# A delta-rule layer whose instructions are written in another order: the chain of the recurrence first, one shared PSUM bank in one fixed sequence

## The reference

```python
a = lmat + eye                       # per chunk, unit lower triangular; lmat from k k^T, decay, beta
sol = solve_triangular(a, rhs)       # rhs: beta v and beta k exp(g)
intra = where(tril, (q @ k.T) * decay, 0)
def step(state, inp):                # one chunk after the other
    v_new = uc - wc @ state
    out = (qc * exp(gc)) @ state + ac @ v_new
    state = state * exp(g_last) + (kc * exp(g_last - gc)).T @ v_new
    return state, out
o = o_fwd + o_bwd
o = o * rsqrt(mean(o * o) + EPS) * out_norm * silu(z)
```

## Time and profile before

| | us |
|---|---|
| three runs: lowest, median, highest | 2757.07, 2758.05, 2759.13 |
| the profiled execution | 2765.49 |
| its span, first to last instruction | 2763.5 |
| mean granted TensorE clock in it | 0.968 of full speed |
| the seven rounds of the delta layer, 2138.25 to 2338.00 | 199.8 |

### The profile page before, as it was taken

How to read it: one execution, slowest core, us unless ns; L and a number is a source line. 1 busy time by engine, 2 the same in 40 slices (tenths; PEclk the granted TensorE clock), 3 DMA queues, 4 the chain that set the end, 5 groups by cost and what they waited for, 6 DMA issues and landing times.

```text
span 2763.5 us, 32840 instructions
## 1 busy us (share of the span) xinstructions
PE 2574.3 (93%) x12894; PEld 2107.8 (76%) x12894; DVE 1379.9 (50%) x2344; ACT 1097.8 (40%) x1898; POOL 342.5 (12%) x535
## 2 busy tenths in 40 slices
PE   5979999999999989889999999999998888999998
PEld 3767777778766767778967888888776887888887
DVE  5667567466464655653234533325776434443322
ACT  4355342353353545444363422215544443422222
POOL 2233011001200013110000000001023520000000
PEclk9989999999999999999999999999998889999999
DMA  5522265246410421143201333334323000333332
GB/s 220 183 76 70 92 220 173 84 139 190 134 35 29 133 73 47 45 126 92 69 1 37 109 97 94 99 96 150 92 61 67 25 26 5 92 100 97 93 99 76
DMA packets 155521, 258.83 MB, mean 94 GB/s; under 512 B 20367, under 2 KB 73642, under 8 KB 154345
## 3 DMA queue, kind: packets, MB, share of 16 engines
q1 hardware_dynamic: 134992, 201.62, 23.2%
q0 software_dynamic: 18128, 53.46, 6.0%
q10 hardware_dynamic: 2249, 1.65, 0.2%
HBM read 249.78 MB, written 10.02 MB: 94 GB/s over the span
## 4 chain that ended last, share of the span: by engine, by line
PE 75%; DVE 10%; ACT 8%; DMA 3%; POOL 2%; issue 2%; SPq 0%; ACTq 0%; DVEq 0%; POOLq 0%
PE PS L219 19%; PE PS L220 19%; PE PS L221 19%; PE PS L979 2%; PE PS L1807 2%; ACT tmp L746 2%; PE PS L1584 1%; PE PS L1603 1%; PE PS L1823 1%; DVE dn_qkvT L2873 1%; DVE x L802 1%; DVE w_lo L211 1%; DVE macc L490 1%; DVE hT_lo L814 1%; PE PS L1593 1%
## 5 line engine op out<-in xcount | busy, mean ns | idle before, releaser
L204 ACT ACTIVATE w_hi<-w_raw 128x1024 fp32r<-128x1024 f32 (+1 forms) x348 | 357.8, 1035 | 1062.1 <-DMA w_raw<-in_ffn_w_gate_up 308.1
L211 DVE TENSOR_TENSOR w_lo<-w_raw,w_hi 128x1024 fp32r<-128x1024 f32 (+1 forms) x348 | 412.3, 1194 | 723.0 <-ACT w_hi L204 721.6
L219 PE MATMUL PS<-hT_hi,w_hi 128*128 128x512 f32 (+1 forms) x1600 | 611.4, 382 | 27.0 <-DVE hT_lo L814 18.9
L221 PE MATMUL PS<-hT_hi,w_lo 128*128 128x512 f32 (+1 forms) x1600 | 603.2, 377 | 0.0
L220 PE MATMUL PS<-hT_lo,w_hi 128*128 128x512 f32 (+1 forms) x1600 | 603.0, 377 | 0.0
L219 PE MATMUL PS<-w_hi,hT_hi 128*128 128x512 f32 (+1 forms) x864 | 349.7, 405 | 30.9 <-ACT gla_szT L1048 8.3
L219 PEld LDWEIGHTS PS<-hT_hi,w_hi 128*128 128x128 f32 x1600 | 307.7, 192 | 86.0 <-issue 25.2
L221 PEld LDWEIGHTS PS<-hT_hi,w_lo 128*128 128x128 f32 x1600 | 307.0, 192 | 54.3
L220 PEld LDWEIGHTS PS<-hT_lo,w_hi 128*128 128x128 f32 x1600 | 307.6, 192 | 51.9 <-issue 0.2
L220 PE MATMUL PS<-w_lo,hT_hi 128*128 128x512 f32 (+1 forms) x864 | 340.0, 394 | 0.0
L221 PE MATMUL PS<-w_hi,hT_lo 128*128 128x512 f32 (+1 forms) x864 | 339.5, 393 | 0.0
(11 more groups left out here) (610 smaller groups left out, 3459.5 us busy)
## 6 DMA issues: line engine op xcount, KB each, us to landing
w_raw<-in_ffn_w_gate_up SPq DMA_DIRECT2D x176, 256.0 KB, 3.1
mraw<-in_w_mod POOLq DMA_DIRECT2D x160, 256.0 KB, 3.9
w_raw<-in_gla_w_in SPq DMA_DIRECT2D x48, 512.0 KB, 4.6
w_raw<-in_ffn_w_down SPq DMA_DIRECT2D x44, 512.0 KB, 3.7
w_raw<-in_fox_w_in SPq DMA_DIRECT2D x32, 512.0 KB, 3.8
w_raw<-in_sgu_w_in SPq DMA_DIRECT2D x24, 512.0 KB, 4.9
w_raw<-in_dn_w_in SPq DMA_DIRECT2D x24, 512.0 KB, 3.8
w_raw<-in_gla_w_out SPq DMA_DIRECT2D x16, 512.0 KB, 4.5
```

The source lines that it names most:

```text
L204: nc.scalar.activation(w_hi[:, n % NS, :, 0:m], w_raw[:, n % NS, :, 0:m], ACT.Copy).then_inc(w_hidone, 1)
L211: nc.vector.tensor_tensor(w_lo[:, n % NS, :, 0:m], w_raw[:, n % NS, :, 0:m], w_hi[:, n % NS, :, 0:m].bitcast(F32), ALU.subtract).then_inc( ...
L219: nc.tensor.matmul(o, l_hi, r_hi, start=start, stop=False)
L221: return nc.tensor.matmul(o, l_lo, r_hi, start=False, stop=stop)
```

## The change

The arithmetic is the same. The loop bodies of PE, ACT and DVE are written in another order, the waits are fitted to it, and a few buffers move:

- The scores go to bank 7 instead of bank 1, which gives bank 7 one fixed sequence in a round: lengths and length rows of head h - 2, v turned, k turned, scores.
- In a round PE starts with hop 1 of chunk 0 and `right(h, 0)`; `decay_rows` moves from the first place to the middle, `scores` from third to near the end, behind `turn(h, 1)`. `right` no longer waits for `dn_AT`.
- The first `turn` takes banks 2 and 3 before `decay_rows` does; the second `turn` therefore waits for the two exponentials that read the decay rows there (`eg`).
- Lengths, square root and output of a head come one round later than before (head h - 2 in round h), the last head's behind the loop.
- The keys of the second direction are decayed on DVE (`decayed_key`, 4 instructions), no longer on ACT.
- The second inverse of heads 3 to 5 has a place of its own, so SP's load of it waits for the recurrence only at h = 2.
- POOL's order is unchanged; in `decayed_query` the count of `prep` becomes 3 h + 3, since the scores are now third to count there.

```diff
@@ positions and waits on PE
                 def decay_rows(h):
                     for d in range(2):
-                        if h:
-                            t_.wait_ge(q.te, B.te + 5 * h)
+                        t_.wait_ge(q.te, B.te + 5 * h + d + 1)
...
                 def scores(h):
-                    if h:
-                        t_.wait_ge(q.pc, B.pc + 4 * h)
+                    t_.wait_ge(q.kte, h + 1)
+                    t_.wait_ge(q.D, 3 * h + 3)
                     for c in range(TT):
-                        mm = t_.matmul(PS[:, 1, cs(c)], r.qkvT[:, HP + HO[h], cs(c)], ...
+                        mm = t_.matmul(PS[:, 7, cs(c)], r.qkvT[:, HP + HO[h], cs(c)], ...
...
-                            t_.wait_ge(q.at, 2 * h + 2)
+                            if h:
+                                t_.wait_ge(q.pc, B.pc + 4 * h)
...
+                            if n == 1:
+                                t_.wait_ge(q.eg, 2 * h + d + 1)
...
@@ PE, the loop
                 for h in range(NH + 1):
...
-                    if inv:
-                        decay_rows(h)
                     if rec:
-                        recur(h - 1, 0, 0)
                         recur(h - 1, 0, 1)
                     if inv:
-                        scores(h)
...
                         right(h, 0)
...
+                    if h >= 2:
+                        lengths(h - 2)
...
+                    if inv:
+                        decay_rows(h)
+                        turn_k(h)
+                    if rec:
+                        recur(h - 1, 2, 0)
+                    if inv:
+                        right(h, 1)
+                    if h == 0:
+                        chunk_matrix(5, (4, 5, 6))
...
+                    if inv:
+                        turn(h, 1)
+                    if rec:
                         recur(h - 1, 2, 2)
                     if inv:
-                        right(h, 1)
+                        scores(h)
...
@@ ACT, the loop
+                        a.wait_ge(q.prep, 3 * h + 2)
+                        for c in range(TT):
+                            ins = a.activation(r.qkvT[:, 2 * HP + HO[h], cs(c)], PS[:, 7, cs(c)], ...
+                        ins.then_inc(q.kte, 1)
+                        rows_exp(0)
                     if rec:
                         value_new(h - 1, 2)
                     if inv:
                         right_out(h, 1)
-                        turned_out(h, 1)
+                        rows_exp(1)
...
@@ POOL
                 def decayed_query(h):
...
-                    p.wait_ge(q.prep, 3 * h + 1)
+                    p.wait_ge(q.prep, 3 * h + 3)
...
@@ DVE, the loop
                     if rec:
                         state(h - 1, 0)
...
+                    if h >= 2:
+                        output(h - 2)
+                    if inv:
+                        decay(0)
+                    if rec:
+                        residual(h - 1, 2)
+                    if inv:
+                        decay(1)
+                        decayed_key()
...
+                    if inv:
+                        weights(1)
                         merge(h, 1)
                     if rec:
-                        output_lengths(h - 1)
+                        gated(h - 1)
+                length_recip(NH - 1)
+                normed(NH - 1)
                 output(NH - 1)
```

More of the change, by code:

```diff
@@ L2501, in recur @@
                         if hop == 0:
[L2502 to L2508, removed]
                             if c == 1 and d == 0:
@@ L2524, in recur @@
                         else:
+                            if c == 0 and d == 0:
+                                if h:
+                                    t_.wait_ge(q.oy, B.oy + 3 * h - 2)
+                                t_.matmul(PS[:, 6, :], r.zr[0:1, :], r.zr[0:1, 0:1].to_broadcast([1, S]), start=True, stop=False)
+                                t_.wait_ge(q.at, 2 * h + 2)
                             t_.wait_ge(q.ve, i + 1)
@@ L2636, in pe @@
                     if inv:
-                        turn(h, 1)
-                    if h == 0:
-                        chunk_matrix(5, (4, 5, 6))
+                        left(h, 1)
                     if rec:
@@ L2642, in pe @@
                     if inv:
-                        left(h, 1)
+                        turn(h, 2)
                     if rec:
                         recur(h - 1, 3, 2)
-                        lengths(h - 1)
-                    if inv:
-                        turn(h, 2)
-                    if rec:
-                        length_rows(h - 1)
+                lengths(NH - 1)
+                length_rows(NH - 1)
                 t_.wait_ge(q.os, B.os + KT)
@@ L2752, in act, with rows_exp, root @@
                     p = h % 2
-                    if inv:
-                        for d in range(2):
-                            a.wait_ge(q.D, 2 * h + d + 1)
-                            if d == 0 and h:
-                                a.wait_ge(q.qg, 2 * h)
-                            a.activation(ajunk[:] if d == 0 else qg_at(h), PS[:, 2 + d, :], ACT.Exp).then_inc(q.eg, 1)
+                    def rows_exp(d):
+                        a.wait_ge(q.D, 3 * h + d + 1)
+                        if d == 0 and h:
+                            a.wait_ge(q.qg, 2 * h)
+                        a.activation(ajunk[:] if d == 0 else qg_at(h), PS[:, 2 + d, :], ACT.Exp).then_inc(q.eg, 1)
+                    def root(n):
+                        a.wait_ge(q.head, 3 * n + 2)
+                        a.activation(stat[:, 40:44], PS[:, 7, 0:TT], ACT.Sqrt, scale=1.0 / P, bias=eps[:]).then_inc(q.root, 1)
                     if rec:
@@ L3012, in dve, with decay @@
                     p = h % 2
-                    if h >= 2:
-                        output(h - 2)
-                    if inv:
-                        for d in range(2):
-                            v.wait_ge(q.gr, 2 * h + d + 1)
-                            for c in range(TT):
-                                ins = v.scalar_tensor_tensor(out=d_.AT[:, p, d, cs(c)], in0=PS[:, 2 + d, cs(c)],
-                                                             scalar=r.G[:, d, c, HO[h]:HO[h] + 1], in1=r.cm[:, d, :],
-                                                             op0=ALU.subtract, op1=ALU.add)
-                            ins.then_inc(q.D, 1)
+                    def decay(d):
+                        v.wait_ge(q.gr, 2 * h + d + 1)
+                        for c in range(TT):
+                            ins = v.scalar_tensor_tensor(out=d_.AT[:, p, d, cs(c)], in0=PS[:, 2 + d, cs(c)],
+                                                         scalar=r.G[:, d, c, HO[h]:HO[h] + 1], in1=r.cm[:, d, :],
+                                                         op0=ALU.subtract, op1=ALU.add)
+                        ins.then_inc(q.D, 1)
@@ L3023, in dve @@
                     if rec:
                         state(h - 1, 0)
-                    if inv:
-                        v.wait_ge(q.prep, 3 * h + 1)
-                        for d in range(2):
-                            v.wait_ge(q.Dx, 2 * h + d + 1)
-                            v.tensor_tensor(d_.AT[:, p, d, :], d_.AT[:, p, d, :], PS[:, 1, :], ALU.mult).then_inc(q.at, 1)
+                    if h >= 2:
+                        length_recip(h - 2)
                     if rec:
                         residual(h - 1, 1)
-                        state(h - 1, 1)
-                        residual(h - 1, 2)
+                    if h >= 2:
+                        normed(h - 2)
```

122 lines of the change are left out of this document (70 added, 52 removed).

## The result

The changed kernel takes 2772.8 us (median of 5, 2767.1 to 2773.1); timed beside it, the one before takes 2758.05. The ratio is **1.0043, 95% interval [1.0025, 1.0061]**: 11.9 us slower, between 6.9 and 16.8. A second timing gave 1.0037 [1.0023, 1.0050]. Forecast: 2766.0 us, +8.0, slower.

A forecast was written before the change was run, and what follows sets the result against it. The chain runs through round 0 to POOL's transfers, POOL's solve, then PE's rounds 3 to 6 and tail. 9.6 - 4.8 + 3.3 = 8.1 us later; 2758.05 + 8.0 = 2766.0 us, range 2757.5 to 2773.5.

The forecast's parts named there:

- Part 1: Round 0, POOL's start: 24 block transfers wait behind decayed_query(0) for the scores, ending 9.6 us later.
- The bounds: Round 0's lateness: 9.1 us with PE at full clock from the start, 11.6 with underrated waits on ACT.
- Part 2: POOL's chain from last issue to toe keeps its 58.3 us; decayed_query(1) has 5 us of cover; right(3, 0) at 2248.6.
- Part 3: Rounds 3 to 5: 24.7 us each at full clock, plus slow-clock time; 4.8 of the 9.6 us won back.
- the wait that I had named: Mid-round on PE: turn(h, 1) waits for ACT's second decay exponential, costing 0.25 + 1.55 us.
- the 1.5 us for rounds 4 and 5: Slow-clock allowance on PE for rounds 4 and 5 together, 1.5 us.
- Part 4: Round 6 and tail: head 4's work now stands between the hops, +3.3 us, bounds 1.5 and 4.5; tail unchanged.
- its items: Round 6: square and product +1.0, lengths and length rows +0.9 and +0.8, output's cast and subtraction +0.6 us.
- rival 1: Rounds 3 to 5 have no slow stretches, round 6 costs half: +2.0 us, or 2760; chance 0.22.
- rival 2: Rounds don't get shorter, 27.8 us each, through ACT's middle wait or a hop: +12.9 us, 2771; chance 0.14.
- rival 3: POOL's solve is interrupted, waiting for round 1's scores, for instance 4 us: +12, 2770; chance 0.06.
- rival 4: The 24 issues don't hold the solve, issue and making overlap as before: -6.0 us, 2752; chance 0.04.

The follow-up runs named there:

- e1a: Changed kernel with POOL's 24 block transfers and load back ahead of decayed_query(0): layer 206.35 us, ratio 1.0027 to the kernel before.
- e3: e1b with ACT's second decay exponential right behind the first: layer 196.09 us, ratio 0.9990 to the kernel before.
- e4: Changed kernel with 70 constant products on PE while it waits in round 3: layer 206.84 us, ratio 1.0025 to the kernel before.
- e7: e3 with head 4's lengths, root and output later in round 6: layer 195.82 us, ratio 0.9998 to the kernel before.
- e1b: e1a with decayed_query(1) after 16 steps of the solve instead of 10: layer 201.36 us, ratio 1.0003 to the kernel before.
- e5: e3 with 30 constant products on PE while it waits in round 3: layer 191.27 us, ratio 0.9996 to the kernel before.
- e6: e3 with POOL issuing 8 of SP's 24 transfers of solved blocks: layer 195.50 us, ratio 0.9997 to the kernel before.
- e10: e5 run once more, unaltered: layer 190.78 us, ratio 0.9991 to the kernel before.
- e8: e5 with e7's order in round 6: layer 195.39 us, ratio 0.9984 to the kernel before.
- e11: e8 with 36 constant products in round 3 instead of 30: layer 197.10 us, ratio 0.9985 to the kernel before.
- e2: Kernel before, with POOL waiting for all matrices of heads 3 to 5 ahead of decayed_query(0): layer 213.43 us, ratio 1.0042.

## Why the prediction was right in sum, and where its terms were off

**Part 1, +9.6 forecast, +6.7 measured; the mechanism is shown.** The 24 issues took 13.1 us as worked out, behind `decayed_query(0)`. The scores came earlier than I put them. Against line 2348's issue, `right(0, 0)` stood at 3.1 us, where I had 4.5: I took the landing of the earlier trace rows with 4.4, and it was 2.9 in this execution. DVE's part of the third matrix stood at 28.5 against my 31.3. So 1.4 of the 2.9 us is the landing; the rest is spread over PE's way from the first to the third matrix, where I had underrated the pace. The bounds (9.1 to 11.6) didn't hold it, and the lower one was wrongly worked out: I let the third matrix cut 3 us of faster pace to 0.5, but only the last 8 of the 24 issues need it, and they begin 8.7 us behind the first. Uncut, the bound is 6.6.

**Part 2, right.** From last issue to `right(3, 0)` I had 61.6 us and it took 62.0; the second `decayed_query` waited for nothing, with 2.1 us of cover (scores done by 2198.9, first product of POOL at 2201.04) where I had 5. e1a shows what happens without it.

**Part 3, -4.8 forecast, -3.1 measured.** A round at full clock: 24.7 forecast, 24.64 measured, and e3 removes 1.07 of it by removing the wait that I had named. The mis-sized term is the clock behind the idle stretch: 3.0 us forecast, 6.0 measured (30.68 against 24.64), and e4 takes 6.2 away. On the other side the 1.5 us for rounds 4 and 5 didn't come: the granted clock was 1.00 in both. With part 2's 0.4 that makes 1.9; three rounds at 24.64 instead of 24.7 take 0.2 off, and 1.7 is what the stretch lacks. The Trainium skill (TensorE: Matmul & The Clock Gate, Part 1), by which the array drops to half rate when idle and comes back after sustained work, agrees in kind: 17.33 us idle, then 1.94 us for eight products that take 1.00 from 2260 on.

**Part 4, +3.3 forecast, +4.2 measured.** To the last output product it is 12.72 us (2326.56 to 2339.28) against 9.39 before: +3.33, as forecast, though its items weren't measured one by one; e7 gives 1.3 of it back by moving head 4's work. The rest is the last transposes (line 2549) at 2.07 us instead of 1.22: half pace again, which I had not counted in the tail.

**The sum.** +8.1 forecast and +7.8 measured in the layer, from errors of -2.9, +1.7 and +0.9 that nearly cancel. The path through POOL's issues and the signs of the parts were right; that the sum is so close is luck. The rivals: rival 1's rounds without slow stretches are refuted for round 3 and true for 4 and 5; rival 2 is refuted (24.64); rival 3 didn't occur in the changed kernel; rival 4 is what e1b makes by hand, and there the loss goes, but not below: I had priced it at -6.0 us with no slow stretch, and e1b, whose round 3 starts at half pace too, has -0.3 in the layer. e3 has -5.5.

**What stays open.** The timed differences are 3 to 4 us above those of the layer for the changed kernel (11.9 and 10.2 against 7.8 and 7.2), and gains of 6 to 11 us in the layer (e5, e6, e7, e10) are timed at 0.6 to 2.5. The intervals, some 3 us either way, cover the first but not all of the second. One reading fits most: the one profiled execution of before may hold a layer that is some us longer than its usual one, and the kept clock may fail in other executions, as it did in e8 and e11. e2 fits it less well: 11.8 in the layer and 11.6 timed, though 2.1 of the 11.8 are the half pace behind hop 1 of round 6, and without them it is 9.7. No second profile of before was made, so this isn't shown. The order of the kernels and the causes of the changed kernel's loss don't hang on it.

## What to carry to other kernels

Before rating a faster loop body, ask which queue outside it sets when the next stage may start: here rounds got 3.2 us shorter each, but the chain ran through POOL's issues, and an order on PE that makes the scores late held 24 transfers whose data had long been there. A small instruction that waits for another engine must not stand ahead of a row of issues; and when it is moved, look where its next copy in the same queue will wait (e1a lost 5.2 us that way). The idle stretch ahead of round 3 cost twice, once as wait and once as half pace behind it.

## What the runs showed of the hardware

- **Half pace outlasts the idle stretch.** After 17.33 us without work PE ran 12.9 us at half pace; after 7.81 us (e3) it still ran about 11.8 us so, and round 3 took 29.05 us instead of 23.57. I had read 3 us from the kernel before, whose idle stretch was 4.31 us.
- **Constant products kept the pace in three executions of five.** It stayed full where they ran up to the real work (e4) and where 1.03 and 1.24 us were left (e10, e5); it halved with 1.56 us left (e8) and with 2.95 (e11). Five executions don't make a rule.
- **Issues took longer side by side.** SP's issue of the same transfer took 0.43 us alone (e3) and 0.57 beside POOL's (e6), one execution each.
